# A two-block transformer kernel: the first loads in another order, fewer warm-up multiplications, and the small steps of both mixing parts moved ahead of weight splits

## The chip, the cores and the metric

The kernel runs on 1 core of one Trainium2 chip. The metric is the device time of one execution in microseconds (us), of which the median of several executions is taken. TensorE is called PE below (its weight loads PEld), VectorE DVE, ScalarE ACT, GpSimd POOL, and SyncE, which only issues transfers here, SP.

## The reference, cut to what matters

Two transformer blocks run one after the other on one sequence of 256 rows of 1024 float32 values.

```
h = x
h = h + 0.5 * swiglu(rms_norm(h), ffn1...)            # F0: 1024 -> 2816 -> 1024
h = h + mixer(rms_norm(h), ...)                       # M0: block attention + stick-breaking attention
h = h + 0.5 * swiglu(rms_norm(h), ffn2...)            # F1
x = rms_norm(h, final_norm)
x = x + 0.5 * swiglu_ffn(x, ffn1_2...)                # F2
x = x + mixer_2(rms_norm_2(x), ...)                   # M1: fox_attention + dsa_attention (top 64 keys)
x = x + 0.5 * swiglu_ffn(x, ffn2_2...)                # F3
```

In the second mixer `fq` and `fk` are normed by head with `rms_norm_2` and multiplied with each other for the "fox" heads, whose logits get `cum` differences and a causal mask. `dk` is normed too. A score from `iq` and `ik`, weighted by `iw`, picks the 64 best keys of each row for the "dsa" heads.

## The kernel before

**Tiles and units.** All products are in float32r. A weight w is split into `w_hi` (the rounded value, made by ACT in `split_hi`, L729) and `w_lo` = w - `w_hi` (made by DVE in `split_lo`, L1108), and an activation likewise into `xT_hi` and `xT_lo`. Each product is three multiplications: hi by hi, hi by lo, lo by hi. Weights come in *units* of 128 x 2048 values (1 MB, two transfers) into 6 landing buffers `raw`; there are 4 buffers `w_hi` and 6 `w_lo`. SP issues the transfers of all units in the order of use and waits for a free buffer (`free`, a wait on `unit_used`). PE waits for `lo_done` before it uses a unit.

**Stages.** F0, M0, F1, F2, M1 and F3 follow each other. PE multiplies through all of them, and the other engines prepare its operands beside it.

**The start (F0).** `warm_up` (L1656 to L1661) makes `WARM[0]` = 4 multiplications of zeros, waits for the identity and the first gain row, turns the gain row (L1659), and makes `WARM[1]` = 12 more. Then `first_turn(0)` waits for the first half of x (columns 0 to 511), turns it (L1670, 8 transposes), ACT makes `xT_hi` (L745), and `first_columns(0, 0)` multiplies with the first 256 columns of unit 0 (L1694), for which DVE rounds the weights (L1159) and takes the rest (L1161). Then come `first_turn(1)` on x's second half, `first_columns(0, 1)`, `(1, 0)` and `(1, 1)`, each 24 multiplications of 256 columns.

**The mixing parts.** The work of M0 and M1 is cut into *slots*, four to a projection j: PE in slot s does 12 multiplications (narrow in slots 4 to 7 of M1) of one half unit and row block, then the small items of the slot. A table `items_of(b)` puts the items in slots by number. "TR" turns the rows of a name and a half (`qa`, `ka`, ... ; `fq`, `dk`, `fk` in M1), "SM" and "SB" are the scores of a head, "IX" the scores of the index, "CU" the sums for `cum`. One slot later ACT takes the rounded part of a TR (`turn`, L926 to L939) and DVE the remainder (`turn_rest`, L1493 to L1506), and only then is the score bank free again: items use banks 4 and 5 in turn, so that each item waits for the reader of the last but one (`score_bank`). In each slot every engine goes through a fixed list of steps. On DVE, `split_lo` stands in odd slots ahead of `turn_rest`; on ACT, `split_hi` stands in even slots behind `turn`.

**Norms by head in M1.** ACT squares (`square_heads`), DVE sums (`mean_heads`, L1332), ACT guesses the inverse root (`guess_heads`), DVE refines it and scales `fq` (`norm_heads(0)`, slot 16), `dk` (`norm_dk`, slot 16) and `fk` (`norm_heads(1)`, slot 18; L1343 to L1358). DVE also runs eight rounds of the top-64 search (`top_round`, L1460 to L1464) in slots 15 and 22 to 28.

**POOL** adds the causal mask to the spread `cum` rows (L690, eight additions) as soon as those have landed; the fox heads (slots 21 to 28 on PE) wait for it one slot later on DVE.

**Slots by the trace.** In M1 slot 16 of PE ends with the transposes of `fq0` at 807.4 us, slot 17 with `dk` at 810.6, slot 18 with `fq1` at 815.2, slot 19 with `fk0` at 818.4, slot 20 with `fk1` at 822.0, slot 22 with the second fox head at 829.4, slot 32 with the second dsa head at 870.1. Slot 20 is the first that uses unit 10 of M1, whose `w_lo` is called `w_lo5`.

Of the kernel before, what the change touches and what calls it, by code (L numbers as in the profile page):

```python
# [49 lines left out]
WARM = (4, 12)  # L50
# [53 lines left out]
def items_of(b):  # L104
    if b == 0:
        out = [(10, "TR", ("qa", 0)), (11, "TR", ("ka", 0)), (12, "TR", ("qa", 1)), (15, "TR", ("ka", 1))]
        out += [(t, "SM", ("moba", h)) for h, t in enumerate((13, 14, 16, 17, 18, 20, 21, 22))]
        out += [(19, "TR", ("qb", 0)), (23, "TR", ("kb", 0)), (24, "TR", ("qb", 1)), (26, "TR", ("kb", 1))]
# [75 lines left out]
def build(nc, a, out):  # L184

    ctx = ExitStack()
    with ctx:
# [352 lines left out]
        def _(sp):  # L540
            def load_x(n):

                c = slice(n * NB, (n + 1) * NB)
                for tt in range(TT):
                    sp.dma_start(x[:, tt, c], a["x"][0, tt * P:(tt + 1) * P, c]).then_inc(x_in[n], 16)
# [33 lines left out]

            for ph in PHASES:  # L580
# [37 lines left out]
        def _(pool):  # L618
# [8 lines left out]
            for n in range(2):  # L627
                pool.wait_ge(x_in[n], 16 * 2)
# [58 lines left out]
            pool.wait_ge(cum_in, 48)  # L687
            for h in range(NH):
# [26 lines left out]
        def _(act):  # L715
# [148 lines left out]
            def mixer(b):  # L864
# [149 lines left out]
                for slot in range(LAST_SLOT):  # L1014
# [44 lines left out]
                    if q in (0, 2) and slot > 0:  # L1059
                        for u in next_units(ph, j)[q // 2:q // 2 + 1]:  # L1060
                            split_hi(u)
                    if slot in (41, 42, 44, 45):

                        if slot == 41:
                            act.wait_ge(gated if b == 1 else evac_dve, 8)
                        g_rows = gate[:, (slot - 1) % 2 if slot < 44 else slot % 2, (slot // 44) * DM:(slot // 44 + 1) * DM]
                        act.activation(g_rows, g_rows, ACT.Sigmoid).then_inc(sigmoid, 1)
                    if slot == 40:
                        act.preload_act_table_set("sigmoid_and_others")
# [13 lines left out]
            act.dma_start(ident, a["consts"][:, 0:P]).then_inc(ident_in, 16)  # L1083
            act.dma_start(gain_rows, a[gains[0]].rearrange("(k p) -> k p", p=P)).then_inc(gain_row_in, 16)
            for tt in range(TT):
                act.dma_start(x[:, tt, 0:NB], a["x"][0, tt * P:(tt + 1) * P, 0:NB]).then_inc(x_in[0], 16)
# [9 lines left out]
        def _(dve):  # L1096
# [198 lines left out]
            def mixer(b):  # L1295
# [238 lines left out]
                rounds = {t: k for k, t in enumerate((15, 22, 23, 24, 25, 26, 27, 28)[:TOPK // 8])}  # L1534
                for slot in range(LAST_SLOT):
# [26 lines left out]
                    if q in (1, 3) and 1 < slot < 42:  # L1562
                        for u in next_units(ph, j)[q // 2:q // 2 + 1]:
                            split_lo(u)
                    if b == 1:
                        if slot in (14, 17):
                            mean_heads((slot - 14) // 3)
                        if slot == 18:
                            norm_heads(1)
# [525 lines left out]
```

## Time and profile before

| | |
|---|---|
| time, median of 3 executions | 1139.14 us (1139.08 to 1139.6) |
| time of the profiled execution | 1138.66 us |
| its span, first to last instruction | 1136.9 us |
| PE busy | 1123.3 us |
| DVE, ACT, POOL busy | 773.6, 621.5, 64.7 us |
| granted TensorE clock, mean | 1.000 |

The 1.8 us between span and time lie outside the instructions. PE is idle for 13.6 us of the span. By stretches of the trace these are 3.5 us before 22 us, 1.0 us between 235 and 430 (M0), 0.8 us between 430 and 620, 3.6 us between 620 and 830 and 1.5 us between 830 and 1000 (M1), and 3.4 us at the end, from 1000 us on.

### The profile page before, as it was taken

To read this page: it belongs to the slowest core of one execution; us is meant where nothing else is said; L and a number is where in the kernel's file an instruction comes from. 1 tells how busy PE (TensorE), PEld (TensorE's weight loads), DVE (VectorE), ACT (ScalarE), POOL (GpSimd) and SP (SyncE) were. 2 spreads that over 40 slices of the span, in tenths; PEclk is the share of its full clock that TensorE was granted. 3 is DMA by queue.
4 is the path that set the end of the run, shared out by engine and by line. 5 is a ranking of instruction groups with operands and counts; after the bars stand their busy time and mean duration, and the time that the engine had idled before them with its cause. 6 is when DMAs were issued, how large, how long until landed. Compare 5 with 4: busy or idle time off the path is not lost.

```text
span 1136.9 us, 15038 instructions
## 1 busy us (share of the span) xinstructions
PE 1123.3 (99%) x5933; PEld 961.8 (85%) x5933; DVE 773.6 (68%) x1070; ACT 621.5 (55%) x843; POOL 64.7 (6%) x105
## 2 busy tenths in 40 slices
PE   8999999999999999999999999999999999999998
PEld 7888888888888888888888888888788888888887
DVE  6777754754887777775487777457987487777742
ACT  5655533677557456554365555337677764655530
POOL 1000000100000000000000000030354100000000
PEclk9999999999999999999999999999999999999999
DMA  9765565654454565555555555556643445555551
GB/s 323 227 193 185 185 239 188 206 159 138 158 175 167 167 216 191 186 186 186 193 195 185 185 187 187 203 157 241 204 142 119 138 158 185 187 185 185 185 185 38
DMA packets 142614, 208.04 MB, mean 183 GB/s; under 512 B 9328, under 2 KB 100616, under 8 KB 142544
## 3 DMA queue, kind: packets, MB, share of 16 engines
q1 hardware_dynamic: 139008, 197.48, 52.2%
q0 software_dynamic: 3088, 9.00, 2.5%
q8 instruction: 47, 0.77, 0.3%
q10 hardware_dynamic: 448, 0.59, 0.2%
q14 instruction: 23, 0.19, 0.1%
HBM read 205.98 MB, written 2.65 MB: 184 GB/s over the span
## 4 chain that ended last, share of the span: by engine, by line
PE 91%; ACT 4%; DVE 3%; issue 2%; DMA 0%; ACTq 0%; DVEq 0%
PE banks L1759 25%; PE banks L1626 15%; PE banks L1628 15%; PE banks L1627 15%; PE banks L1757 13%; DVE w_lo L1108 1%; PE banks L1694 1%; ACT w_hi L729 1%; PE banks L1648 1%; DVE stat L1506 1%; PE banks L1907 1%; PE banks L1934 1%; PE banks L1935 1%; PE banks L1933 0%; ACT twice L938 0%
## 5 line engine op out<-in xcount | busy, mean ns | idle before, releaser
L1108 DVE TENSOR_TENSOR w_lo<-raw,w_hi 128x2048 fp32r<-128x2048 f32 x186 | 424.1, 2283 | 176.0 <-ACT w_hi L729 175.8
L729 ACT ACTIVATE w_hi<-raw 128x2048 fp32r<-128x2048 f32 x186 | 352.9, 1899 | 112.1 <-PE banks L1628 112.0
L1759 PE MATMUL banks<-xT,w_hi 128*128 128x512 f32 x1280 | 313.7, 392 | 0.0
L1759 PEld LDWEIGHTS banks<-xT,w_hi 128*128 128x128 f32 x1280 | 232.9, 189 | 43.1
L1626 PE MATMUL banks<-w_hi,xT 128*128 128x512 f32 (+1 forms) x464 | 183.5, 395 | 0.0
L1628 PE MATMUL banks<-w_hi,xT 128*128 128x512 f32 (+1 forms) x464 | 179.6, 387 | 0.0
L1627 PE MATMUL banks<-w_lo,xT 128*128 128x512 f32 (+1 forms) x464 | 179.3, 386 | 0.0
L1757 PEld LDWEIGHTS banks<-xT,w_lo 128*128 128x128 f32 x1280 | 169.9, 191 | 9.5
L1757 PE MATMUL banks<-xT,w_lo 128*128 128x256 f32 x1280 | 173.7, 283 | 0.0
L1626 PE MATMUL banks<-w_hi,hT_hi 128*128 128x512 f32 x352 | 137.5, 391 | 0.0
L1628 PE MATMUL banks<-w_hi,hT_lo 128*128 128x512 f32 x352 | 137.2, 390 | 0.0
L1627 PE MATMUL banks<-w_lo,hT_hi 128*128 128x512 f32 x352 | 137.1, 390 | 0.0
L807 ACT ACTIVATE gate<-gate 128x256 f32<-128x256 f32 x80 | 33.5, 418 | 158.1 <-DVE gate L1233 158.1
L1628 PEld LDWEIGHTS banks<-w_hi,xT 128*128 128x128 f32 x464 | 87.2, 188 | 18.4
L1627 PEld LDWEIGHTS banks<-w_lo,xT 128*128 128x128 f32 x464 | 87.5, 189 | 15.2
L1626 PEld LDWEIGHTS banks<-w_hi,xT 128*128 128x128 f32 x464 | 87.4, 188 | 15.0
L1626 PEld LDWEIGHTS banks<-w_hi,hT_hi 128*128 128x128 f32 x352 | 66.1, 188 | 14.2 <-issue 0.6
L1628 PEld LDWEIGHTS banks<-w_hi,hT_lo 128*128 128x128 f32 x352 | 66.1, 188 | 13.7
L1627 PEld LDWEIGHTS banks<-w_lo,hT_hi 128*128 128x128 f32 x352 | 66.1, 188 | 13.6
L1231 DVE TENSOR_TENSOR gate<-banks,gate 128x512 f32<-128x512 f32 x80 | 55.1, 688 | 17.4 <-ACT gate L801 17.1
L801 ACT ACTIVATE gate<-banks 128x512 f32<-128x512 f32 x80 | 47.7, 597 | 31.9 <-PE banks L1759 31.8
L1239 DVE TENSOR_TENSOR gate<-gate 128x256 f32<-128x256 f32 x80 | 34.1, 426 | 38.8 <-ACT gate L807 38.8
(304 smaller groups left out, 936.1 us busy)
## 6 DMA issues: line engine op xcount, KB each, us to landing
raw<-in_ffn_w_gate SPq DMA_DIRECT2D x88, 512.0 KB, 3.7
raw<-in_ffn_w_up SPq DMA_DIRECT2D x88, 512.0 KB, 4.7
raw<-in_ffn_w_down SPq DMA_DIRECT2D x88, 512.0 KB, 4.2
raw<-in_w_in SPq DMA_DIRECT2D x76, 512.0 KB, 4.5
raw<-in_w_out SPq DMA_DIRECT2D x16, 512.0 KB, 4.3
raw<-in_w_branch_moba SPq DMA_DIRECT2D x4, 512.0 KB, 4.9
raw<-in_w_branch_sb SPq DMA_DIRECT2D x4, 512.0 KB, 6.4
raw<-in_w_branch_a SPq DMA_DIRECT2D x4, 512.0 KB, 3.9
```

Of the source, the lines that this page charges most:

```text
L729: act.activation(w_hi[u % SLOTS][:, 0:n], raw[u % RAWS][:, 0:n], ACT.Copy).then_inc(hi_done, 1)
L801: act.activation(low_part, banks[:, b:b + 2, SEQ:NB], ACT.Copy).then_inc(low_copied, 1)
L807: act.activation(r, r, ACT.Silu).then_inc(pair_silu, 1)
L1108: dve.tensor_tensor(w_lo[r][:, 0:n], raw[r][:, 0:n], w_hi[u % SLOTS][:, 0:n], ALU.subtract).then_inc(lo_done, 1)
L1231: dve.tensor_tensor(r, banks[:, b:b + 2, 0:SEQ], low_part, ALU.add).then_inc(pair_summed, 1)
L1239: dve.tensor_tensor(r[:, 0, :], r[:, 0, :], r[:, 1, :], ALU.mult).then_inc(pair_h, 1)
L1506: ins = dve.scalar_tensor_tensor(lo, src, f, hi, ALU.mult, ALU.subtract)
L1626: pe.matmul(dst, st(hi), mhi, start=start, stop=False)
L1627: pe.matmul(dst, st(hi), mlo, start=False, stop=False)
L1628: return pe.matmul(dst, st(lo), mhi, start=False, stop=stop)
L1757: m = pe.matmul(bank[b + s][:, 0:SEQ], ml, xT_hi[:, k, :], start=False, stop=False)
L1759: m = pe.matmul(bank[b + s], mh, xT[:, k].rearrange("p a s -> p (a s)"), start=k == 0, stop=k == KC - 1)
```

## The change

1. Start. SP issues the identity, then all of x's first half in one transfer, ahead of the first weights; x's second half is one transfer too. ACT keeps only the gain row. `WARM` becomes (4, 2).
2. M0. In the table, `ka1` goes from slot 15 to 14, and the moba heads from (13, 14, 16, 17, 18, 20, 21, 22) to (13, 15, 16, 17, 19, 20, 21, 22), `qb0` from 19 to 18. In slot 13 DVE's remainder goes ahead of the split.
3. M1. Remainders go ahead of the splits in all slots. The splits of DVE's slots 9 and 17 move one slot on, and so does ACT's split of slot 20. The remainder of `fq0` goes ahead of the sums of slot 17, `norm_heads(1)` ahead of all else in slot 18.
4. M1. POOL's masks wait for `norm_dk` (`rows_ready` 5). The first top-64 round goes from slot 15 to 20.
5. Both mixing parts. ACT loads the table for Sigmoid in slot 41, behind the copies and ahead of the first Sigmoid, where it was at the end of slot 40.

```diff
-WARM = (4, 12)
+WARM = (4, 2)
...
-        out = [(10, "TR", ("qa", 0)), (11, "TR", ("ka", 0)), (12, "TR", ("qa", 1)), (15, "TR", ("ka", 1))]
+        out = [(10, "TR", ("qa", 0)), (11, "TR", ("ka", 0)), (12, "TR", ("qa", 1)), (14, "TR", ("ka", 1))]
...
-                for tt in range(TT):
-                    sp.dma_start(x[:, tt, c], a["x"][0, tt * P:(tt + 1) * P, c]).then_inc(x_in[n], 16)
+                sp.dma_start(x[:, :, c], a["x"][0].rearrange("(t p) d -> p t d", p=P)[:, :, c]).then_inc(x_in[n], 16)
...
+            sp.dma_start(ident, a["consts"][:, 0:P]).then_inc(ident_in, 16)
+            load_x(0)
...
             pool.wait_ge(cum_in, 48)
+            pool.wait_ge(rows_ready, 5)
...
-                    if q in (0, 2) and slot > 0:
-                        for u in next_units(ph, j)[q // 2:q // 2 + 1]:
-                            split_hi(u)
+                    for t in ((slot,) if b == 0 or slot not in (20, 21) else (slot - 1,)):
+                        if t % 4 in (0, 2) and t > 0:
+                            for u in next_units(ph, t // 4)[t % 4 // 2:t % 4 // 2 + 1]:
+                                split_hi(u)
...
                         if slot == 41:
+                            act.preload_act_table_set("sigmoid_and_others")
                             act.wait_ge(gated if b == 1 else evac_dve, 8)
...
-                    if slot == 40:
-                        act.preload_act_table_set("sigmoid_and_others")
...
-            act.dma_start(ident, a["consts"][:, 0:P]).then_inc(ident_in, 16)
...
-            for tt in range(TT):
-                act.dma_start(x[:, tt, 0:NB], a["x"][0, tt * P:(tt + 1) * P, 0:NB]).then_inc(x_in[0], 16)
...
-                rounds = {t: k for k, t in enumerate((15, 22, 23, 24, 25, 26, 27, 28)[:TOPK // 8])}
+                rounds = {t: k for k, t in enumerate((20, 22, 23, 24, 25, 26, 27, 28)[:TOPK // 8])}
...
+                        if slot == 18:
+                            norm_heads(1)
+                    rests = [it for it in ITEMS[b] if it.kind == "TR" and slot - it.slot == 1]
+                    ahead = b == 1 or slot == 13
+                    for it in rests if ahead else ():
+                        turn_rest(it)
+                    if b == 1 and slot == 17:
+                        mean_heads(1)
+                    t = slot - 1 if b == 1 and slot in (9, 10, 17, 18) else slot
+                    if t % 4 in (1, 3) and 1 < t < 42:
+                        for u in next_units(ph, t // 4)[t % 4 // 2:t % 4 // 2 + 1]:
+                            split_lo(u)
+                    for it in rests if not ahead else ():
+                        turn_rest(it)
```

SP's transfers at the very start, before (`raw` is a landing buffer of weights):

```order
0 L539 UNCONDITIONAL_BRANCH
1 L553 DMA raw<-in_ffn_w_gate 128x4x256
2 L553 DMA raw<-in_ffn_w_up 128x4x256
3 L545 DMA x<-in_x 128x512 x2
4 L553 DMA raw<-in_ffn_w_gate 128x4x256
5 L553 DMA raw<-in_ffn_w_up 128x4x256
```

and now, with the identity (`const`) and x's first half in front:

```order
0 L539 UNCONDITIONAL_BRANCH
1 L579 DMA const<-in_consts 128x128
2 L544 DMA x<-in_x 128x2x512
3 L552 DMA raw<-in_ffn_w_gate 128x4x256
4 L552 DMA raw<-in_ffn_w_up 128x4x256
5 L544 DMA x<-in_x 128x2x512
```

What stood on ACT's queue, the identity and 512 KB of x, now stands ahead of the first weights.

DVE in M1, slots 16 to 19, before. `xg` and `norm_cols` rows are the norms by head, `dk_rows` the norm of dk, `stat0` the remainder of `fq0`, `dk_rest` that of dk, `w_lo5` the split of unit 10:

```order
709 L1358 COPY dk_rows<-dk_rows 128x2x64 [waits dve_chain]
710 L1108 TENSOR_TENSOR w_lo5<-raw5,w_hi1 128x2048 [waits hi_done]
711 L1332 TENSOR_REDUCE norm_cols<-gate 128x16 [waits heads_squared]
712 L1335 TENSOR_SCALAR norm_cols<-norm_cols 128x16 [waits heads_summed]
713 L1506 SCALAR_TENSOR_TENSOR stat0<-banks,hg,stat0 64x2x256 [waits qk_hi]
714 L1506 SCALAR_TENSOR_TENSOR stat0<-banks,hg,stat0 64x2x256
715 L1343 SCALAR_TENSOR_TENSOR norm_cols<-norm_cols 128x16 [waits heads_guessed]
```

and now, from the same norm of dk on:

```order
705 L1357 COPY dk_rows<-dk_rows 128x2x64 [waits dve_chain]
706 L1505 SCALAR_TENSOR_TENSOR stat0<-banks,hg,stat0 64x2x256 [waits qk_hi]
707 L1505 SCALAR_TENSOR_TENSOR stat0<-banks,hg,stat0 64x2x256
708 L1331 TENSOR_REDUCE norm_cols<-gate 128x16 [waits heads_squared]
709 L1334 TENSOR_SCALAR norm_cols<-norm_cols 128x16 [waits heads_summed]
710 L1342 SCALAR_TENSOR_TENSOR norm_cols<-norm_cols 128x16 [waits heads_guessed]
711 L1343 TENSOR_TENSOR norm_cols<-norm_cols 128x16 [waits dve_chain]
712 L1344 SCALAR_TENSOR_TENSOR norm_cols<-norm_cols 128x16 [waits dve_chain]
713 L1348 TENSOR_TENSOR xg<-xg,norm_cols 128x512 [waits dve_chain]
714 L1348 TENSOR_TENSOR xg<-xg,norm_cols 128x512
715 L1492 SCALAR_TENSOR_TENSOR dk_rest<-banks,hg,dk_twice 64x256 [waits zeroed,qk_hi]
717 L1107 TENSOR_TENSOR w_lo5<-raw5,w_hi1 128x2048 [waits hi_done]
```

The split of unit 10 went from the place right behind the norm of dk to one behind the remainders of `fq0` and dk and the whole norm of fk.

## Rows read from the trace of the kernel before

**Rows 1.** Page, part 1: engines, busy us, instructions.
```profile
PE 1123.3 (99%) x5933; PEld 961.8 (85%) x5933; DVE 773.6 (68%) x1070; ACT 621.5 (55%) x843; POOL 64.7 (6%) x105
```

**Rows 2.** PE's waits, all: line, releaser, us in total, times, longest.
```profile
PE banks L1933 <- ACT probT L985: 1.0, 2, 0.7
```

**Rows 3.** Timeline of PE in M0: start, us, what, [idle before, releaser].
```profile
242.19 0.30 PE L1892 MATMUL banks<-twice,stat 128*128 128x128 f32 x1 [0.28 <-DVE stat L1506]
```

**Rows 4.** Timeline of PE in M1, small items that waited, and slot 19's.
```profile
785.32 0.33 PE L1892 MATMUL banks<-twice,stat 128*128 128x128 f32 x1 [0.33 <-DVE rest L1496]
...
807.37 0.66 PE L1861 MATMUL banks<-const,xg 128*128 128x128 f32 x4 [0.76 <-DVE xg L1349]
...
815.18 0.63 PE L1861 MATMUL banks<-const,xg 128*128 128x128 f32 x4 [1.42 <-DVE stat L1506]
...
818.41 0.60 PE L1861 MATMUL banks<-const,xg 128*128 128x128 f32 x4
...
822.02 0.63 PE L1861 MATMUL banks<-const,xg 128*128 128x128 f32 x4 [0.24 <-DVE stat L1506]
...
829.41 0.30 PE L1892 MATMUL banks<-twice,stat 128*128 128x128 f32 x1 [0.82 <-DVE rest L1506]
...
870.11 0.30 PE L1892 MATMUL banks<-dk_twice,stat 128*128 128x128 f32 x1 [0.82 <-DVE stat L1506]
```

**Rows 5.** Timeline of PE at the start.
```profile
5.10 4.74 PE L1661 MATMUL banks<-hT_lo 128*128 128x512 f32 x12
...
11.36 1.38 PE L1694 MATMUL banks<-w_hi,xT 128*128 128x256 f32 x8 [0.65 <-ACT xT L745]
...
15.28 1.20 PE L1694 MATMUL banks<-w_hi,xT 128*128 128x256 f32 x8
```

**Rows 6.** Timeline, first microseconds: SP's first transfer, POOL behind x, DVE's rounding.
```profile
0.74 0.44 SPq L553 DMA_DIRECT2D raw<-in_ffn_w_gate  x1
...
5.41 0.69 DVE L1159 CAST w_hi<-raw 128x1024 fp32r<-128x1024 f32 x1
...
9.48 0.10 POOL L629 MEMSET small<- 128x1 f32 x1 [9.04 <-DMA x<-in_x]
```

**Rows 7.** Transfers issued between 0.7 and 0.9 us: KB each, us to landing.
```profile
raw<-in_ffn_w_gate SPq DMA_DIRECT2D x1, 512.0 KB, 4.3
```

**Rows 8.** Fifth to sixth us: PE, PEld, DVE, ACT, POOL busy, PEclk, DMA, GB/s.
```profile
5.00:6.00 1.00, 1.00 (x3) 0.88 (x4) 0.75 (x2) 0.00 (x0) 0.00 (x0) 1.00 1.09 371
```

**Rows 9.** Timeline of PE, two narrow windows within the twelve warm-up multiplications.
```profile
5.70 1.91 PE L1661 MATMUL banks<-hT_lo 128*128 128x512 f32 x4
...
8.68 1.16 PE L1661 MATMUL banks<-hT_lo 128*128 128x512 f32 x4
```

**Rows 10.** Timeline of DVE in M1, slots 16 to 19.
```profile
805.47 1.84 DVE L1349 TENSOR_TENSOR xg<-xg,norm_cols 128x512 f32<-128x512 f32 x2
...
812.07 1.21 DVE L1332 TENSOR_REDUCE norm_cols<-gate 128x16 f32<-128x1024 f32 x1
...
813.52 1.51 DVE L1506 SCALAR_TENSOR_TENSOR stat<-banks,hg,stat 64x512 fp32r<-64x512 f32 x2
...
815.70 1.29 DVE L1349 TENSOR_TENSOR xg<-xg,norm_cols 128x512 f32<-128x512 f32 x2
817.03 0.98 DVE L1493 SCALAR_TENSOR_TENSOR dk_rest<-banks,hg,dk_twice 64x256 fp32r<-64x256 f32 x2
818.04 2.29 DVE L1108 TENSOR_TENSOR w_lo<-raw,w_hi 128x2048 fp32r<-128x2048 f32 x1
```

**Rows 11.** Timeline of ACT in M1: `fq0` in slot 17, table load of slot 40.
```profile
808.06 1.39 ACT L939 ACTIVATE stat<-banks,hg 64x512 fp32r<-64x512 f32 x2 [0.56 <-PE banks L1861]
...
905.00 1.28 ACT L1069 ACT_TABLE_LOAD   x1
```

**Rows 12.** Timeline of POOL in M1, the first four masks.
```profile
805.63 3.66 POOL L690 TENSOR_TENSOR gate<-gate,const 128x256 f32<-128x256 f32 x4 [7.25 <-DMA cum_last<-cum_rows]
```

More of the change, by code:

```diff
@@ L105, in items_of @@
     if b == 0:
-        out = [(10, "TR", ("qa", 0)), (11, "TR", ("ka", 0)), (12, "TR", ("qa", 1)), (15, "TR", ("ka", 1))]
-        out += [(t, "SM", ("moba", h)) for h, t in enumerate((13, 14, 16, 17, 18, 20, 21, 22))]
-        out += [(19, "TR", ("qb", 0)), (23, "TR", ("kb", 0)), (24, "TR", ("qb", 1)), (26, "TR", ("kb", 1))]
+        out = [(10, "TR", ("qa", 0)), (11, "TR", ("ka", 0)), (12, "TR", ("qa", 1)), (14, "TR", ("ka", 1))]
+        out += [(t, "SM", ("moba", h)) for h, t in enumerate((13, 15, 16, 17, 19, 20, 21, 22))]
+        out += [(18, "TR", ("qb", 0)), (23, "TR", ("kb", 0)), (24, "TR", ("qb", 1)), (26, "TR", ("kb", 1))]
         out += [(t, "SB", ("sb", h)) for h, t in enumerate((25, 27, 28, 30, 31, 33, 34, 36))]
@@ L627, in _ @@
             for n in range(2):
-                pool.wait_ge(x_in[n], 16 * 2)
+                pool.wait_ge(x_in[n], 16)
             pool.memset(freq[:, 0:1], INV_FREQ[0]).then_inc(gained, 4)
@@ L1561, in mixer @@
                             norm_dk()
[L1562 to L1567, printed above, removed]
                         if slot == 18:
                             norm_heads(1)
+                    rests = [it for it in ITEMS[b] if it.kind == "TR" and slot - it.slot == 1]
[10 more added lines that the diff above has]
+                        turn_rest(it)
+                    if b == 1 and slot == 14:
+                        mean_heads(0)
                     for it in ITEMS[b]:
@@ L1573, in mixer @@
                             accumulate(it)
-                        if it.kind == "TR" and d == 1:
-                            turn_rest(it)
                         if it.kind == "TY" and d == 1:
@@ L1663, in first_turn @@
             def first_turn(n):
-                pe.wait_ge(x_in[n], 16 * 2)
+                pe.wait_ge(x_in[n], 16)
                 for j in (2 * n, 2 * n + 1):
```

## The prediction, made before the changed kernel ran

> **What bounds the kernel now.** I read part 1 of the page first: PE is busy for 1123.3 of 1136.9 us [rows 1]. No work is removed from it but ten warm-up multiplications, so that a gain can only come out of the 13.6 us in which it is idle, and out of the start, where the warm-ups count as busy and produce nothing. Next I read the table of PE's waits. The reader sees there that no wait repeats: each is one place in a mixing part, of 0.3 to 1.4 us; the largest entry for ACT is two waits on `probT`, 1.0 us in all, 0.7 the longest [rows 2]. Then the timelines of PE at those places. In M0 it waits 0.28 us for the remainder of `qa1` [rows 3]. In M1 it waits 0.33 us (remainder of `ik`), 0.76 (norm of `fq`), 1.42 and 0.24 (remainders that hold the score bank), 0.82 (remainder of `fk1`) and 0.82 (remainder of `dq1`) [rows 4]. That is 4.39 us in M1. The change moves DVE's steps at just these places.
>
> **The start.** Before, PE reached its first real multiplication at 11.36 and the second quarter of the first chunk at 15.28 us [rows 5]. Both halves of x had landed by 9.48 us, where POOL's wait for both ends [rows 6]; the twelve warm-ups lasted to 9.84 [rows 5], so they covered the wait for x and cost little themselves. The first transfer on SP's queue, 512 KB, was issued at 0.74 [rows 6] and landed 4.3 us later [rows 7]. Now x's half has nearly that place, one short issue (0.44 us) behind: I put it at 1.2 + 4.3 = 5.5 us. The first weights come 512 KB later; at 371 GB/s [rows 8] that is 1.4 us, so 6.9. DVE rounds them in 0.69 [rows 6], so 7.6. The transposes of x and ACT's copy are done by then (the 8 transposes and the first copy took 1.7 us before, 9.68 to 11.36), so PE starts its columns at about 7.65, 3.7 us earlier than at 11.36.
>
> Not all of this is kept, because of the clock. PEclk reads 1.00, that is 2.4 GHz, from the first us on [rows 8], but the warm-ups themselves show the lower level: four of them from 5.70 last 1.91 us, that is one per 0.427 us (less the tail of 0.63), which is 512 columns at 1.2 GHz; the last four start within 0.76 us of each other, one per 0.25 [rows 9]. So PE went up only at about 8.7 us, after nine of the twelve, back to back since 5.10. Now there are two, then a wait for x, 8 transposes, a wait for weights; PE will begin its columns at the lower level. A 256-column multiplication then takes half of 0.427, 0.213 us, against 0.12 (8 started within some 0.85 us when the stream ran). Of the 24 of the first quarter I charge 18 at the lower level and 6 at the upper, 3.8 + 0.7 = 4.6 us, between the ends of none and all 24 (5.1). PE is then done at 12.2, the turn of x's second half takes the 0.8 us it took before, and the second quarter starts at 13.0 instead of 15.28: **2.3 us gained**. With none at the lower level DVE's remainder of the weights (1.23 us) and of x hold the quarter until about 11.1: 3.4 gained. With all 24 and more of the next, and the first weights 1.2 us later than I put them, nothing is left, or up to 0.5 lost. Later weights need nothing new: the same bytes stand ahead of them, and no PE wait stands between 15 and 235 us that could grow.
>
> On this the Trainium skill has a rule that speaks against the change, in "TensorE: Matmul & The Clock Gate", section Part 1 on the HAM clock gate: the array is throttled by default, and activity releases it. By this rule alone, cutting ten warm-ups takes away the release; the trace agrees so far as the warm-ups did run slow until 8.7 us. If the level stayed low through all 24, the gain would be 1.8 instead of 2.3.
>
> **M0.** `qa1`'s remainder (1.4 us) goes ahead of the 2.3 us split in slot 13, and the item behind it is now `ka1`, not a head. The 0.28 us goes [rows 3]. Moving a head away from ACT's full slot after `qb0` should free the smaller of the two `probT` waits, some 0.4 of 1.0 us [rows 2]. The split is needed three slots, 10 us, later: covered. The first head's softmax now stands behind the split, about 1 us later, with as much to spare: I take **0.6 gained**, from -0.4 to 0.7.
>
> **M1.** (a) `ik`'s remainder ahead of unit 6's split: 0.33 goes; the split lands 2 us later and is used at slot 12, 7 us on. (b) Without the top-64 round (1.4 us) and without masks beside it, `norm_heads(0)` ends about 2 us before PE asks, so 0.76 goes. The round in slot 20 lies in DVE time before the remainder of `fk1`. (c) `fq0`'s remainder ahead of the sums and of unit 10's split: 1.42 goes, and 0.24 behind it. (d) `fk1`'s remainder ahead of unit 12's split, and ACT's split behind `fk1`: 0.82 goes. (e) `dq1` the same: 0.82 goes. (f) The Sigmoid table (1.28 us, 905.00) [rows 11] stood in front of the last head's copy; behind it, the 0.7 wait goes [rows 2]. Sum 4.39 + 0.66 = 5.05.
>
> Against it stands one new wait. Unit 10's split now comes after `fq0`'s remainder, the sums, `norm_heads(1)` and dk's remainder. DVE can begin with `fq0` only when ACT has turned it: ACT's copy of 1.39 us started at 808.06 behind PE [rows 11], now at about 807.2, when its own split ends; so 808.6. Then 1.51 (remainder), 1.21 and 0.2 (sums), 0.5 (ACT's guess), 0.65 and 1.29 (norm of fk), 0.98 (dk), 2.29 (split) [rows 10] with their gaps: 817.35. PE came to slot 20's multiplications at 818.41 + 0.35 = 818.76 [rows 4]; without the waits before it (0.33 + 0.76 + 1.42 = 2.51) it would come at 816.25. **A wait of 1.15 us is new**, at the first multiplication of slot 20. Its lower end is 0.3 (ACT's copy straight behind PE), its upper end 1.8: the xg step costs 1.84 instead of 1.29 where masks run beside it [rows 10]. DVE then still has time for `fk0` and `fk1`: I place the latter's remainder at 825.7, PE's question at 827.0. So M1 gains 5.05 - 1.15 = **3.9 us**, between 1.5 (two of the six waits stay in another form) and 4.7.
>
> The masks: before, the first four lasted 3.66 us from 805.63 [rows 12], now they wait for dk's norm at about 805.8, so they hardly move; what moves is DVE's norm, out of their way. Behind them only the fox heads wait (823 us and later, masks done by 812 to 814.5): no cost. The Trainium skill, "SBUF — State Buffer", section on two separate sides, says that a DVE step with two SBUF inputs and a reading GpSimd step take a shared port pair from each other for a whole instruction. The trace agrees: 1.84 against 1.29 for the same step, and no change for those that read PSUM or one tile. By this rule the new time of the masks falls on remainders and sums that do not need the pair.
>
> **The sum.** 2.3 + 0.6 + 3.9 = 6.8 us. The profiled execution took 1138.66, its span 1136.9; it becomes 1131.9 with a span of 1130.1. The median stands 0.48 above the profiled one: 1132.3 us.
>
> **Rivals.**
> - *A, the clock.* The lower level lasts through the second quarter too, 48 multiplications. 48 x 0.093 = 4.5 us against 3.7: the start loses 0.8, and the total gain is 3.7: 1135.4. For it: the idle pieces between x, ACT and the weights; against: slow multiplications fill their own gaps, so PE is without a break from 7.65 on.
> - *B, DVE in slot 20.* Masks and DVE meet in the norm of fk and the split of unit 10 runs to 819; the wait is 2.7 instead of 1.15, and half of the rest comes back at slot 22: 1134.0. For it, 1.84 against 1.29; against, the masks begin while DVE is idle for 2.7 us and should be done by 812.
> - *C, the queue.* One transfer for both row blocks of x lands no sooner than the separate ones did, 6.9 us after issue, so 8.1; the start gains 1 instead of 2.3, and the change does not do there what it says: 1133.6.
> - *D, slower.* The clock stays at the lower level until the end of the first chunk, because the columns wait again and again for weights that now come 1.4 us later. 96 x 0.093 = 8.9 us against 3.7 at the start; with M0 and M1 this ends near 1139.8. It decides from about 88 slow multiplications on. Against it: before, the level held from 8.7 on through a pause of 0.65 us [rows 5].
>
> **How the numbers follow.** Forecast 0.58, A 0.14, B 0.14, C 0.10, D 0.04. The best corner (3.4 + 0.7 + 4.4 = 8.5) gives 1130.6, the slow end of A with a weak M1 some 1136.6; I give 1130.0 to 1136.6. A measurement of this kernel can tell 0.2%, 2.3 us, so faster begins below 1136.9. Faster 0.88, within 0.2% 0.07 (from A and B together with lost waits), slower 0.05 (D and its like).
>
> **What would show it.** Right: PE's columns begin near 7.7 us with starts 0.21 us apart, then 0.12; the second quarter starts near 13; in M1 there is one wait of about 1.2 us on `w_lo` near the start of slot 20 and none at `fq0`, `fq1`, `fk1`, the second fox and the second dsa head; the last `probT` wait is gone. Wrong: starts 0.21 apart beyond 15 us (A, D); x's wait ending at 8 us (C); DVE's split of unit 10 longer than 2.5 us or ending more than 11.5 us after `fq0`'s turn (B); a remainder still ahead of PE in M1.

## The result, and the profile of the changed kernel

| | us, median (lowest to highest) | runs |
|---|---|---|
| before | 1139.14 (1138.77 to 1139.86) | 6 |
| changed | 1130.11 (1129.00 to 1130.85) | 6 |

The ratio is 0.9919, 95% interval 0.9906 to 0.9932: 9.2 us faster where 6.8 was forecast. Scaled by the ratio, the time is 0.9919 x 1139.14 = 1129.9 us, 0.1 us below the lower end of the range; the median itself lies 0.1 us inside it. The profiled execution took 1129.47 us, its span 1127.7.

The page's part 1 of the changed kernel, to set beside [rows 1]:

```profile
PE 1119.9 (99%) x5923; PEld 960.6 (85%) x5923; DVE 770.7 (68%) x1070; ACT 621.5 (55%) x843; POOL 60.1 (5%) x105
```

PE is idle for 7.8 us of its span, before 13.6. All of PE's waits in the changed kernel (line, releaser, us in total, times, longest); before, M1 alone had seven:

```profile
PE banks L1661 <- DVE hT_lo L1150: 1.5, 1, 1.5
PE banks L1631 <- DVE w_lo L1107: 1.2, 1, 1.2
PE banks L1776 <- DVE gate L1205: 0.8, 1, 0.8
PE banks L1699 <- DVE w_hi L1158: 0.4, 1, 0.4
PE banks L1892 <- DVE stat L1505: 0.3, 1, 0.3
PE banks L1675 <- DMA x<-in_x: 0.3, 1, 0.3
```

The second row is new and stands in M1; the third stood in the second FFN before as well, and so did the fifth, in M0 (now at 292.60 us). Every wait of M1 in [rows 2, 4] is gone. The start, PE alone, to set beside [rows 5]:

```profile
3.67 1.22 PE L1666 MATMUL banks<-hT_lo 128*128 128x512 f32 x2
5.15 1.97 PE L1675 MATMUL banks<-const,x 128*128 128x128 f32 x8 [0.27 <-DMA x<-in_x]
7.53 2.07 PE L1699 MATMUL banks<-w_hi,xT 128*128 128x256 f32 x8 [0.41 <-DVE w_hi L1158]
9.40 1.57 PE L1699 MATMUL banks<-w_lo,xT 128*128 128x256 f32 x8
10.81 1.12 PE L1699 MATMUL banks<-w_hi,xT 128*128 128x256 f32 x8
11.77 1.03 PE L1675 MATMUL banks<-const,x 128*128 128x128 f32 x8
12.56 1.20 PE L1699 MATMUL banks<-w_hi,xT 128*128 128x256 f32 x8
```

x is turned at 5.15 and the columns start at 7.53. The turns and the first 13 multiplications run at half the clock (1.97 against 1.03 us for eight turns, starts 0.21 us apart instead of 0.12); the rest of the 24 are at full speed. The second quarter starts at 12.56, before at 15.28.

DVE's rows of M1, slots 16 to 19, to set beside [rows 10], and PE behind them in slot 20:

```profile
800.93 0.23 DVE L1357 COPY dk_rows<-dk_rows 128x128 f32<-128x128 f32 x1
804.05 1.51 DVE L1505 SCALAR_TENSOR_TENSOR stat<-banks,hg,stat 64x512 fp32r<-64x512 f32 x2 [2.90 <-ACT stat L941]
805.60 1.22 DVE L1331 TENSOR_REDUCE norm_cols<-gate 128x16 f32<-128x1024 f32 x1
...
808.24 1.29 DVE L1348 TENSOR_TENSOR xg<-xg,norm_cols 128x512 f32<-128x512 f32 x2
809.57 0.98 DVE L1492 SCALAR_TENSOR_TENSOR dk_rest<-banks,hg,dk_twice 64x256 fp32r<-64x256 f32 x2
810.58 2.29 DVE L1107 TENSOR_TENSOR w_lo<-raw,w_hi 128x2048 fp32r<-128x2048 f32 x1
```
```profile
812.93 0.50 PE L1631 MATMUL banks<-w_hi,xT 128*128 128x512 f32 x1 [1.23 <-DVE w_lo L1107]
```

The chain is the one that the prediction wrote down: ACT's copy, `fq0`'s remainder, the sums, ACT's guess, the norm of `fk`, dk's remainder, unit 10's split, PE. DVE stands idle for 2.90 us at its head.

### The profile page after: what moved, and what is told of

The parts are those of the page before. It is cut to its first block, busy times and chain, and to the rows that moved or that the text cites. A ratio compares the mean times of both kernels' runs of the same rounds, so it can differ in the third digit from the quotient of the medians.

```text
span 1127.7 us, 15016 instructions
## 1 busy us (share of the span) xinstructions
PE 1119.9 (99%) x5923; PEld 960.6 (85%) x5923; DVE 770.7 (68%) x1070; ACT 621.5 (55%) x843; POOL 60.1 (5%) x105
## 4 chain that ended last, share of the span: by engine, by line
PE 96%; DVE 2%; ACT 1%; issue 1%; DMA 0%; SPq 0%; ACTq 0%; DVEq 0%
PE banks L1764 26%; PE banks L1631 16%; PE banks L1633 16%; PE banks L1632 16%; PE banks L1762 13%; PE banks L1699 1%; PE banks L1653 1%; PE banks L1912 1%; PE banks L1939 1%; PE banks L1940 1%; DVE w_lo L1107 1%; PE banks L1899 0%; DMA raw<-in_ffn_w_gate 0%; PE banks L1938 0%; PE banks L1866 0%
```

## Where the time went: three stages measured in every trace

The number of PE's instructions is the same in all kernels here, warm-ups aside, so the start of one and the same instruction can be set side by side. Three were taken: the turn of x's second half (14.49 us before), the turn of `iq`'s first part in slot 6 of M1 (774.18), and the last turn behind M1's last streaming multiplications (952.60). Differences between them give what the start, M0 with the FFNs, and M1 gained. Where an edit leaves M0 or M1 alone, that stage agrees with the kernel before to 0.05 us, while the interval of a ratio is 1 us or more wide to each side. The start agrees less well: in the four traces with the old start the second half of x is turned at 14.49, 14.55, 14.76 and 14.85, and the kernel before has the earliest, so that all gains at the start are on the low side, by 0.17 us against the mean of the four. The last of the three, before and changed:

```profile
952.60 0.60 PE L1648 MATMUL banks<-const,xg 128*128 128x128 f32 x4
```
```profile
943.37 0.60 PE L1653 MATMUL banks<-const,xg 128*128 128x128 f32 x4
```

That is 9.23 us: start 2.72, M0 1.42, M1 5.09. The table has all kernels; "gain by ratio" is (1 - ratio) x 1139.1, with an interval of about 1.0 to 1.9 us to each side. "Warm-ups" here and below are those of the second group, `WARM[1]`; the four multiplications of the first group stand in every kernel.

| kernel | median us | ratio (95%) | gain by ratio | start | M0 | M1 |
|---|---|---|---|---|---|---|
| changed | 1130.11 | 0.9919 (0.9906 to 0.9932) | 9.2 | 2.72 | 1.42 | 5.09 |
| changed, again | 1130.10 | 0.9915 (0.9900 to 0.9930) | 9.7 | 2.17 | 1.43 | 5.01 |
| before + start | 1135.89 | 0.9972 (0.9962 to 0.9982) | 3.2 | 3.46 | 0 | 0 |
| before + start, 12 warm-ups | 1136.79 | 0.9978 (0.9969 to 0.9987) | 2.5 | 2.52 | 0 | 0 |
| before + M0 | 1137.60 | 0.9984 (0.9975 to 0.9993) | 1.8 | -0.36 | 1.39 | 0 |
| before + M1 | 1133.93 | 0.9955 (0.9942 to 0.9967) | 5.1 | -0.27 | 0 | 5.11 |
| before + `dq1`'s remainder | 1138.25 | 0.9991 (0.9983 to 1.0000) | 1.0 | -0.06 | 0 | 1.04 |
| changed, no wait of the masks | 1130.08 | 0.9919 (0.9905 to 0.9933) | 9.2 | 1.87 | 1.38 | 5.09 |
| changed, round in slot 15 | 1129.97 | 0.9922 (0.9908 to 0.9935) | 8.9 | 3.40 | 1.43 | 4.47 |
| changed, table in slot 40 | 1131.30 | 0.9933 (0.9920 to 0.9945) | 7.6 | 1.82 | 1.39 | 4.22 |
| changed, unit 10 earlier | 1129.92 | 0.9918 (0.9904 to 0.9931) | 9.3 | 2.28 | 1.43 | 5.29 |
| the same, slots 22 and 27 | 1130.58 | 0.9924 (0.9912 to 0.9936) | 8.7 | 2.13 | 0.33 | 6.16 |
| changed, no warm-up | 1130.98 | 0.9925 (0.9912 to 0.9939) | 8.5 | 1.26 | 1.10 | 5.04 |
| changed, 6 warm-ups | 1129.02 | 0.9910 (0.9896 to 0.9923) | 10.3 | 3.36 | 1.34 | 5.06 |
| 6 warm-ups, unit 10, slot 22 | 1128.27 | 0.9901 (0.9884 to 0.9917) | 11.3 | 2.84 | 1.41 | 6.17 |
| the same, masks later | 1127.52 | 0.9895 (0.9880 to 0.9910) | 12.0 | 2.95 | 1.42 | 6.58 |
| the same, 4 warm-ups | 1127.39 | 0.9893 (0.9879 to 0.9908) | 12.2 | 3.24 | 1.40 | 6.60 |

Within 0.05 us the columns are shown as 0. M0 and M1 repeat to 0.1 us wherever their code is the same (but without warm-ups another 0.3 is lost behind the start of the second turn, in which alone the clock rises: it takes 1.27 us instead of 1.03). The start does not: the eight traces with two warm-ups (the changed kernel, its repeat, the start alone, and the five kernels of M0 and M1 edits on top) gain 1.82 to 3.46.

## Experiments: the three parts alone

**The start alone.** The kernel before with only this:

```diff
-WARM = (4, 12)
+WARM = (4, 2)
+            sp.dma_start(ident, a["consts"][:, 0:P]).then_inc(ident_in, 16)
+            load_x(0)
             for ph in PHASES:
```

> The kernel before with the start's change alone (identity and x's first half ahead on SP's queue, one transfer for both row blocks, two small warm-ups instead of twelve). The prediction's term says 2.3 us (1136.8); the trace after, read at the start of the second quarter, says 2.7 (1136.4) and that all of it is kept to the end, since no PE wait between there and M0 changed. Rival: the start's gain is partly given back later (the stream waits for a weight that lands at a fixed time): then less than 2 us, and a new wait in the first FFN. PE should start its columns near 7.5 us and 16 of 24 at the lower clock level (starts 0.21 apart).

Measured: 3.46 us in the trace, 3.2 by ratio, and all of the gain at the second quarter is there at 952 us. No new wait in the first FFN. But the turns run at half the clock and the columns at the full one from the first; in the changed kernel's trace 13 of the 24 were slow:

```profile
4.94 1.94 PE L1668 MATMUL banks<-const,x 128*128 128x128 f32 x8
7.62 1.22 PE L1692 MATMUL banks<-w_hi,xT 128*128 128x256 f32 x8 [0.74 <-DVE w_hi L1157]
```

So one and the same first 12 us can go two ways. The prediction had this as the upper end of its range (none of the 24 at the lower level: 3.4).

**The same with twelve warm-ups kept.**

> The start's change without the cut of the warm-ups: twelve stand there as before. x lands near 5.5 us, but the warm-ups end at about 9.8, so PE turns x only then, as before (9.68), at the full clock level. If the warm-ups hold PE as this says, 0 to 0.7 us is gained (1138.4 to 1139.1), and the 2.7 us need both edits together. Rival, that the queue alone brings the gain and the warm-ups cost nothing as the forecast's reading of before had it (they covered the wait for x): near 2.7, 1136.4.

Measured: 2.5 us by ratio and by trace. My expectation fell, for a reason that stands in [rows 5]: before, the warm-ups only begin at 5.10, because a product with the gain vector stands in front of them and the vector lands at 4.9. With neither the identity ahead of it nor x behind it on ACT's queue it is there by 3.46 (which of the two held it up, no run tells), and the turns of x begin at 7.17:

```profile
3.67 3.66 PE L1659 MATMUL banks<-hT_lo 128*128 128x512 f32 x12
```

The order of the queues brings most of the gain, then; the cut of the warm-ups brings another 0.9 at best (3.46 against 2.52), and costs 0.35 in the repeat of the changed kernel and 0.70 in the slowest of the eight traces.

**M0 alone** (the two rows of the table of small items, and in slot 13 the remainder ahead of the split):

> The kernel before with M0's change alone: the order of the small items (a head moves away from the turns of ka and qb) and the remainder ahead of the split in slot 13. By the idle shown ahead of PE's instructions, as the prediction took it, 0.28 + 0.38 = 0.6 us (1138.5). By the starts in the trace after, 1.4 us (1137.7), of which the surplus is what a shown idle leaves out, about 0.2 to 0.25 for each of two waits, and 0.4 more that lies in the order of the small items and not in a wait.

Measured 1.39 in the trace, 1.8 by ratio: the size read by starts holds, but the 0.4 that I put down to the order of the small items is mostly a third wait, of 0.27. Three places of the kernel before carry it, each shown here with the streaming multiplication ahead of it:

```profile
241.53 0.39 PE L1628 MATMUL banks<-w_hi,xT 128*128 128x512 f32 x1
...
252.91 0.39 PE L1628 MATMUL banks<-w_hi,xT 128*128 128x512 f32 x1
253.30 0.44 PE L1933 MATMUL banks<-v_a,probT 128*128 128x64 f32 x2
253.57 0.39 PE L1934 MATMUL banks<-v_a,probT 128*128 128x64 f32 x2
...
268.92 0.39 PE L1628 MATMUL banks<-w_hi,xT 128*128 128x512 f32 x1
269.69 0.43 PE L1933 MATMUL banks<-v_a,probT 128*128 128x64 f32 x2 [0.38 <-ACT probT L985]
```
```profile
252.76 0.48 ACT L985 ACTIVATE probT<-banks 128x384 f32<-128x384 f32 x1
```

Where nothing waits, a small item starts 0.23 us behind its multiplication, and the second group of such a head 0.16 behind the first (256.05, 256.28, 256.44 in the kernel with M0's change alone). Here the distances are 0.66 (to 242.19 [rows 3]), 0.39 and 0.27, 0.77 and 0.28. Taken off the undisturbed ones, and with 0.07 for the groups behind the first wait (0.53 against 0.46), the three places lose 0.5, 0.27 and 0.66 us: 1.43 in all against 1.39 measured. The middle one is a wait for `probT`: ACT's copy of it ends at 253.24, and PE goes on 0.06 later, as it does at 269.69. It shows no idle at all, because it lies wholly under the 0.39 us of the multiplication in front.

**M1 alone:**

> The kernel before with M1's change alone (remainders ahead, splits delayed, masks and a top-64 round later, table load behind the copy); start and M0's order as before (the table load is later in both parts). By the idle shown, with the new wait of 1.15, 3.9 us (1135.2). By starts, every one of seven removed waits costs the shown idle plus 0.17 to 0.25, because the multiplication in front of it lasts 0.39 us while the stream starts one each 0.23: 5.0 us (1134.1). The parts should add up: start 2.7, M0 1.4, M1 5.0, together 9.1. If the three gains sum to clearly less than 9.0, part of the gain comes from their combination instead.

Measured 5.11 in the trace, 5.1 by ratio. M0 and M1 add up: 1.39 and 5.11 alone, 1.42 and 5.09 in the changed kernel, so that no part of their gain comes from their combination. With the 2.72 of the changed kernel's own start that is 9.22 against 9.23. Whether the start adds up as closely can't be told, since it differs between executions (3.46 alone, 2.72 and 2.17 in the changed kernel).

**One wait alone.** The kernel before, with `dq1`'s remainder ahead of the split in slot 31 of M1 and nothing else:

> The kernel before with one edit: in slot 31 of M1 dq1's remainder goes ahead of the split. It removes one wait, shown as 0.82 us ahead of the second dsa head. If a removed wait is worth the idle shown ahead of it, 0.82 us; if it is worth the distance of starts that it stretches, 868.89 to 870.11 and 870.64 against 861.60 to 861.83 and 862.28 in the trace after, it is worth 1.07. In the trace the item after this place should come 1.0 to 1.1 us earlier against the kernel before, not 0.8.

Measured 1.04 us in the trace. The ratio, 1.0 us with almost 1 to each side, can't tell 0.82 from 1.07; the trace can. This is the experiment for the term that failed. The waiting place in the kernel before, from the last streaming multiplication to the first behind the item:

```profile
868.89 0.39 PE L1628 MATMUL banks<-w_hi,xT 128*128 128x512 f32 x1
870.11 0.30 PE L1892 MATMUL banks<-dk_twice,stat 128*128 128x128 f32 x1 [0.82 <-DVE stat L1506]
...
870.64 0.40 PE L1626 MATMUL banks<-w_hi,xT 128*128 128x512 f32 x1
```

and without the wait:

```profile
868.97 0.39 PE L1632 MATMUL banks<-w_hi,xT 128*128 128x512 f32 x1
869.19 0.22 PE L1896 MATMUL banks<-dk_twice,stat 128*128 128x128 f32 x1
...
869.65 0.40 PE L1630 MATMUL banks<-w_hi,xT 128*128 128x512 f32 x1
```

1.75 us before, 0.68 after. Idle is counted from the end of the last multiplication, 0.39 us behind its start. In a full stream the next one would have started 0.23 behind it: 0.16 us of the loss lies under the shown duration. Another 0.07 lies behind the wait (0.53 against 0.46 for the item's four groups). The shown 0.82 is 1.05 in truth.

## Experiments: parts of M1 undone

**POOL's wait taken away:**

> The changed kernel without POOL's new wait for dk's norm. In its trace the masks started 7.8 us after the last sums' transfer was issued, against 7.25 in the kernel before, so the wait holds them only about 0.6 us. Theory: no change (within 0.2 us of the changed kernel, 1130.1), since DVE's norm ends at 801.2 with 2.9 us of idle behind it. Rival: the masks then lie beside the last copy of dk and lengthen it (0.23 to 0.70), fq0's head waits; 0.3 to 0.5 us slower.

Measured: M1 5.09, as with the wait. This line of the change is worth nothing in this schedule. Without it the masks start at 802.04, where the last copy of dk ends too (802.06): the sums' transfer lands no sooner, and the 0.6 us that I expected the wait to hold them was not there. The copy takes 0.23 us as before, so the rival fell as well.

**The first top-64 round back in slot 15:**

> The changed kernel with the first top-64 round back in slot 15. It takes 1.44 us of DVE ahead of fq's norm, which then ends at 802.0 instead of 800.57; PE asks at 801.7. Theory: a shown wait of about 0.3 us at fq0's turn, 0.5 by starts, and nothing gained elsewhere, since DVE in slot 20 ends in time: 1130.6. Rival: the round also frees the way for the new wait of slot 20 (no: it stands behind it), so that nothing is lost, 1130.1; or, with masks beside it, 0.76 to 1.1 is back, 1131.1.

M1 gives 4.47 instead of 5.09: 0.62 lost. By starts 0.43 of it is the wait that returns at `fq0`, as the theory says. The other 0.2 was not expected: the wait of slot 20 grows from 1.23 to 1.45, because the masks now run beside a small step of DVE's sums, which takes 0.72 us instead of 0.22, and all behind it in the chain comes later:

```profile
801.38 0.66 PE L1866 MATMUL banks<-const,xg 128*128 128x128 f32 x4 [0.22 <-DVE xg L1348]
...
812.86 0.50 PE L1631 MATMUL banks<-w_hi,xT 128*128 128x512 f32 x1 [1.45 <-DVE w_lo L1107]
```
```profile
806.29 0.72 DVE L1334 TENSOR_SCALAR norm_cols<-norm_cols 128x16 f32<-128x16 f32 x1
```

The median is no help here: 1129.97, faster than the changed kernel's. The start varies by more than the loss; in this profiled execution it gained 3.40.

**The Sigmoid table back in slot 40:**

> The changed kernel with the load of the Sigmoid table back at the end of slot 40, ahead of the last head's copy. By the idle shown in the kernel before (0.66 us in M1, and the larger part of 0.3 in M0) 0.7 to 1.0 us slower; by starts, 905.79 to 906.84 and 907.11 against 897.52 to 897.75 and 897.91 in the changed one, 0.93 in M1 alone: 1131.0 to 1131.4. Rival: what is removed here was made good elsewhere, 1130.1.

M1 gives 4.22, 0.87 lost; M0 loses nothing, where the larger part of 0.3 was expected. The time of 1131.30 lies in the expected range, helped by a start that gained only 1.82. The wait's idle is shown as

```profile
899.44 0.43 PE L1939 MATMUL banks<-dv,probT 128*128 128x64 f32 x2 [0.62 <-ACT probT L987]
```

## Experiments: the new wait, and a better version

**Unit 10's split and `fk`'s sums ahead of `fq0`'s remainder**, in the 2.90 us in which DVE is idle:

```diff
-                    ahead = b == 1 or slot == 13
+                    ahead = b == 1 and slot != 17 or slot == 13
+                    if b == 1 and slot == 17:
+                        mean_heads(1)
                     for it in rests if ahead else ():
                         turn_rest(it)
-                    if b == 1 and slot == 17:
-                        mean_heads(1)
-                    t = slot - 1 if b == 1 and slot in (9, 10, 17, 18) else slot
+                    t = slot - 1 if b == 1 and slot in (9, 10) else slot
```

> The changed kernel with the sums of fk and then unit 10's split ahead of fq0's remainder in slot 17. DVE stands idle for 2.9 us there (801.15 to 804.05), waiting for ACT's copy of fq0; the split (2.29) and the sums fit in and push the remainder to about 806.5. Theory: the new wait at slot 20's first multiplication goes (1.23 shown, 1.4 by starts), fq0's remainder is still ready before PE asks for the score bank at 807.9: 1.4 us faster than the changed kernel, 1128.7. Rival: PE then waits for the score bank at fq1 (the 1.42 of before in a small form) or for fk's norm at 811, and only 0 to 0.7 is gained.

M1 gives 5.29, 0.2 more where 1.4 was the theory; the rival came. The wait of slot 20 is gone and with it 1.47 us between the starts around it (1.23 shown). But 0.40 is lost in front of it and 0.74 behind, and both show as waits:

```profile
811.94 0.63 PE L1866 MATMUL banks<-const,xg 128*128 128x128 f32 x4 [0.24 <-DVE dk_rest L1492]
825.49 0.55 PE L1912 MATMUL banks<-const,prob 128*128 128x128 f32 x3 [0.58 <-ACT prob L952]
```

DVE's rows tell why for the first. Steps of `fk`'s norm that took 0.18 us each in the changed kernel now take 0.45 to 0.67, beside POOL's masks, and the split takes 2.81:

```profile
803.22 2.81 DVE L1107 TENSOR_TENSOR w_lo<-raw,w_hi 128x2048 fp32r<-128x2048 f32 x1
...
808.09 0.67 DVE L1343 TENSOR_TENSOR norm_cols<-norm_cols 128x16 f32<-128x16 f32 x1
808.79 0.66 DVE L1344 SCALAR_TENSOR_TENSOR norm_cols<-norm_cols 128x16 f32<-128x16 f32 x1
```
```profile
801.74 4.88 POOL L692 TENSOR_TENSOR gate<-gate,const 128x256 f32<-128x256 f32 x4 [7.70 <-DVE dk_rows L1357]
```

**With slot 21's split behind the first softening, and in M0 a remainder ahead in slot 27:**

> The same, and with two more moves of DVE: slot 21's split behind fk1's remainder and the softening in slot 22, and in M0 the remainder ahead of the split in slot 27 (a wait of 0.3 us is shown at 292.6 in the trace after). Theory: another 0.3 + 0.2 = 0.5 us for M0, nothing or 0.2 for slot 22: 1128.2. Rival: these moves only shift waits: as the kernel with unit 10's split alone.

M1 6.16: the 0.74 is not lost any more. M0 0.33 instead of 1.43: the shown wait at 292.6 goes (0.46 by starts), and what DVE and ACT do behind the split comes later. In both kernels an ACT split lies in front of a copy that PE needs; in the changed kernel it started at 308.71 and the copy was there in time, here both are 1.7 us later:

```profile
310.40 1.90 ACT L731 ACTIVATE w_hi<-raw 128x2048 fp32r<-128x2048 f32 x1
312.20 0.42 ACT L967 ACTIVATE y_b<-banks 128x128 f32<-128x128 f32 x2
```
```profile
312.60 0.41 PE L1924 MATMUL banks<-soft_hi,tri_r 128*128 128x384 f32 x1 [1.41 <-ACT y_b L967]
```

So a remainder ahead of a split pays only where what stands behind the split has time. In M0's slot 27 it has none, and 1.1 us is lost on balance (0.46 won, 1.54 lost at 312.60).

**Six warm-ups, unit 10's and slot 21's splits moved, M0 as in the changed kernel:**

> The changed kernel with six warm-ups, unit 10's split ahead of fq0's remainder, and slot 21's split moved to slot 22 behind the softening. If slot 21's split is what held the first fox head, the 0.74 us is not lost and M1 keeps 1.46 - 0.40 = 1.06; with 1.1 for the six warm-ups: 1127.9. Rival: the wait appears at the next fox head, 1128.7.

M1 6.17, in all 1128.27. **The same with the masks behind `fk`'s norm:**

```diff
-            pool.wait_ge(rows_ready, 5)
+            pool.wait_ge(rows_ready, 6)
```

> The same, with POOL's masks behind fk's norm instead of dk's. If the masks beside it make the small steps of fk's norm 0.45 to 0.67 us instead of 0.18 and the split 2.81 instead of 2.29, all 1.9 us of that goes, the wait of 0.24 at fk0 with it: 0.4 more, 1127.5. Rival: the steps are slow for another reason, and nothing changes at fk0; or the masks now lie beside something on the path, and a wait of up to 0.5 appears at the fox heads.

M1 6.58: the 0.41 came, no wait is left in M1, and the norm's steps are back at 0.18. The masks take 7.7 us, as in the kernel without this line (5.6 in the changed one), and with time to spare; the split beside them takes 2.92. So where POOL's wait stands is worth 0.4 in this order, and the wait brought nothing in the order of the change.

## Experiments: warm-ups and the clock

**None, six, two again, four:**

> The changed kernel without any warm-up. In its trace two warm-ups start at 3.67 and x is turned at 5.15; 8 turns and 16 of 24 multiplications are at the lower level. Theory: the two do nothing for the clock that the turns and columns don't do themselves, as PE stands idle behind them: same time, within 0.3 us. Rival: without them the level rises later by what they lasted, 1.2 us, that is some 6 to 10 multiplications of 256 columns more at the lower level, 0.093 us each: 0.6 to 0.9 slower.

> The changed kernel with six warm-ups instead of two. At 0.43 us each they last to about 6.3 us, while x has landed at about 5.1: the turns start 1.1 us later, but the first weights are rounded only at 7.5, and 8 turns (1.7 at the lower level) and ACT's copy end near 8.3. Theory: 0.7 us later start, and a clock that rises some 1 us earlier relative to the columns (8 to 12 multiplications fewer at the lower level, 0.7 to 1.1 us): same time or up to 0.4 faster, and a smaller spread of times. Rival: the rise comes with the columns whatever stands ahead: 0.7 slower.

> The changed kernel itself once more, for the spread of its start on one chip with the three kernels beside it. Theory, that with two warm-ups the clock rises in some executions before the columns and in others in the middle of them: times spread over 1.5 to 2 us around 1130.1, and this trace shows the second quarter anywhere between 11.0 and 13.3. Rival, that the spread is one of the chips: all within 0.3 us here.

> The same with four warm-ups, which end at 5.2 us, when x lands, so that PE is neither idle nor held. Theory: the clock has risen by the columns, as with six (same second quarter, 11.0), 0 to 0.2 us faster. Rival: as with two, in some executions it has not, and times spread over 1.5 us with a median 0.5 to 1 above the kernel with six.

Without any, all 24 multiplications of the first quarter start at the lower level, the second turn at 13.23 instead of 11.77, and the start gains 1.26. The theory of no difference fell: by median and ratio the kernel is 0.7 to 0.9 us slower than the changed one, as the rival had it; its trace is 0.6 behind the slowest start of the eight with two warm-ups and 1.46 behind that of the changed kernel. With six the clock is up when x is turned, and the start gains 3.36:

```profile
3.66 2.40 PE L1666 MATMUL banks<-hT_lo 128*128 128x512 f32 x6
5.90 1.03 PE L1675 MATMUL banks<-const,x 128*128 128x128 f32 x8
7.72 1.24 PE L1699 MATMUL banks<-w_hi,xT 128*128 128x256 f32 x8 [0.78 <-DVE w_hi L1158]
```

The turns start 0.75 us later than with two and end earlier; the weights are what the columns wait for. I had expected the same time or up to 0.4 less, and got 1.1 less. All four times lie within 0.15 us (1128.94 to 1129.09). Four warm-ups are as good as six: 1127.28 to 1127.46 against 1127.37 to 1127.77.

With two, the repeat shows a third course: the level was up for the turns (1.09 us), PE then paused 1.71 us for the weights, and from the fifth multiplication on the columns ran at the lower level. Its windows (us, busy time and count of PE, PEld, DVE, ACT, POOL, then PEclk, DMA share, GB/s) have the clock at 0.50, that is 1.2 GHz, in the columns. The kernel without the masks' wait went the same way, behind a pause of 1.88 us:

```profile
5.02 1.09 PE L1675 MATMUL banks<-const,x 128*128 128x128 f32 x8
7.82 1.59 PE L1699 MATMUL banks<-w_hi,xT 128*128 128x256 f32 x8 [1.71 <-DVE w_hi L1158]
9.21 1.95 PE L1699 MATMUL banks<-w_lo,xT 128*128 128x256 f32 x8
```
```profile
7.00:9.00 2.00, 1.18 (x8) 1.18 (x8) 1.89 (x3) 0.82 (x2) 0.00 (x0) 0.86 1.06 390
9.00:11.00 2.00, 2.00 (x11) 2.00 (x11) 2.00 (x6) 0.58 (x1) 0.52 (x2) 0.50 1.11 352
```

The times on that chip spread over 1.5 us (1128.81 to 1130.32), those of the three kernels beside it, with four and six warm-ups, over 0.2 to 0.4. So the spread is not one of the chip. But it doesn't come with two warm-ups alone either: eleven times with twelve (the second kernel above) spread over 1.95 us (1135.64 to 1137.59), and four with two (unit 10 earlier) over 0.4. What sets it stays open.

## Why the prediction was wrong, step by step

- **The start, 2.3 forecast: right.** x turned at 5.15 (5.5), columns at 7.53 (7.65), 13 slow multiplications (18), second quarter at 12.56 (13.0). The eight traces with two warm-ups gain 1.82 to 3.46, the middle of them 2.2; that this is so near the 2.3 is in part luck, since the course of the clock behind it came in only four of the eight. Of the rivals, A, C and D did not come: the level was up before the second quarter in each of the eight, and one transfer for both row blocks landed in time. Not foreseen were that the gain vector comes 1.5 us sooner, and that the course differs between executions.
- **M0, 0.6 forecast: 1.4.** The mechanism was right, both waits went; the size was off. The two shown idles, 0.28 and about 0.4, are 0.5 and 0.66 by starts, and a third wait of 0.27 that no view listed went with them. The gain lies outside the term's own bounds, -0.4 to 0.7.
- **M1, 3.9 forecast: 5.1. This is the step that failed, in its term "5.05".** All seven waits went, as forecast, one by one. The term added the idle shown ahead of PE's instructions. By starts, from the last streaming multiplication ahead of each place to the first behind it, before against changed, the seven are worth 0.59, 0.98, 1.60, 0.42, 1.06, 1.06 and 0.93, together 6.64 instead of 5.05, 0.23 more for each. The single edit of `dq1` shows it by itself: 0.82 shown, 1.04 gained. The upper end of the term was built on the same shown numbers, 4.7, and so it was too low too (the best corner of the whole was even added with 4.4 in its place).
- **The new wait, 1.15 forecast: right.** 1.23 shown at the place named, 1.47 by starts; the prediction's own figures, 817.35 - 816.25, give 1.10. The error of this term was the same, against the other's sign: 6.64 - 1.47 = 5.17, of which 0.08 is lost again in small steps elsewhere.
- **The masks:** they start with the end of dk's norm (801.42, in the changed kernel's time, which is 4.8 us ahead there) and are done at 807.0, in 5.6 us instead of 8.5. B did not come. That their wait costs nothing was right; it also brings nothing. Of what was said of the steps beside them, one part is wrong: those that read one tile did change. Before, beside the masks, the two steps that scale dk took 1.41 us and the copy behind them 0.70; in the changed kernel, ahead of the masks, 0.41 and 0.23. Unchanged were the remainder of `fq0`, which reads PSUM (1.51), and the sums over 1024 columns (1.22).
- **The sum.** The error of the whole is 2.2 to 2.4 us by the median: 1.2 in M1, 0.8 in M0, and the rest within the start's spread.

## What to carry to other kernels

Price a wait on a pipelined engine by the distance of the starts around it against the same place without a wait, not by the idle that the profile shows: here a wait cost 0.13 to 0.28 us more than shown, and one of 0.27 was not shown at all. Compare traces by the starts of the same instruction at the ends of stages; in M0 and M1 that repeats to 0.1 us, where medians whose times spread over 1.5 us can't tell effects of 0.4 us, and once pointed the wrong way. Where a stream is late at its start, let the warm-ups end when the first operands land, and look at several executions: with too few, the clock may rise at a different point in each. And before a step goes ahead of another, look at everything that stands behind the second.

## What the runs showed of the hardware

- PEclk reads 1.00 in the first microseconds of the changed kernel although eight turns take 1.97 us there and 1.03 later. The initial lower level does not show in the column; a fall after it does (0.50 in the repeat). The level has to be read from the distance of starts.
- The same start with two warm-ups took three courses in eight traces: the level up between turns and columns (two traces), up only in the columns (four), or up before the turns and down again in the first columns, behind pauses of 1.71 and 1.88 us (two). With four or six it was up before the columns, and stayed up, in each of the four profiled executions. The Trainium skill, "TensorE: Matmul & The Clock Gate", section Part 1 on the HAM clock gate, has the array throttled until activity releases it; the traces agree, with 1.26 us gained at the start without the second group of warm-ups against 3.36 with six.
- DVE steps of 128 x 16 elements took 0.18 us alone and up to 0.72 beside POOL's masks, the copy of 128 x 128 0.23 and 0.70, and the split of 128 x 2048 2.29 alone and 2.81 to 2.92 beside them. Small steps suffered most in proportion. That each waits for the end of a whole POOL instruction (0.71 us for one mask alone) would fit, but no run here takes it apart.
